# First mixer of a two-block transformer kernel: step size at unit xbc 6, SiLU calls in a row, attention weightings and decay sums further on

## The chip, the cores and the metric

The kernel runs on one core of a Trainium2 chip. The metric is the device time in microseconds; the median of three runs of the kernel before is 944.78 us. A core has TensorE for matmuls, which write to PSUM banks; VectorE, ScalarE and GpSimd for the rest; and queues of DMA transfers. Every engine works through its own instructions in the order in which the program issues them, and they meet only at semaphores. An engine that waits holds up all that is queued behind the waiting instruction.

## The reference

Two blocks, each a token mixer and a feed-forward part, on 256 tokens of width 1024, all in float32. The change lies in the mixer of the first block:

```python
proj = h @ w_in[l]
z, xbc, dt_raw, sb_qkv, nsa_q, nsa_kv, nsa_gate, merge_gate = jnp.split(proj, split_points(), axis=-1)
y_ssm = ssm_mixer(z, xbc, dt_raw, ...)           # state space
y_sb = stick_breaking_attention(sb_qkv)          # w = exp(ls + later), out = w @ v
y_nsa = nsa_attention(nsa_q, nsa_kv, nsa_gate, ...)
...
xbc = jax.nn.silu(causal_dwconv(xbc, conv_w, conv_b))     # in ssm_mixer
dt = jax.nn.softplus(dt_raw + dt_bias)                    # the step size
a = -jnp.exp(a_log)
...
decay = jnp.exp(jnp.where(tri, seg, -jnp.inf))            # per chunk of 128 tokens
w = cb[..., None] * decay * dt_c[:, None]                 # cb = C . B
y = y * silu(z); y = y * rsqrt(mean(y * y) + eps)         # per group of 256
```

The compression branch of `nsa_attention` makes one key and one value of 32 tokens each (`hid`, `kc` in the kernel), and a softmax over 15 of them (`cmp`).

## The kernel before, in words

The projection is cut into units of 256 columns of weights (1 MB each, streamed in through three slots). A float32 weight is split in two parts: ScalarE copies the rounded high part (`w_hi`, L1113), VectorE subtracts it to get the low part (`w_lo`, L1561), and TensorE makes three products for each pair of operands (L480 to L485), 48 matmuls a unit. `ahead(u)` on ScalarE and VectorE issues the splits up to two units on, so a split stands in each engine's queue at the place where the code calls `ahead`. A unit's result lies in one of three PSUM banks `pj`.

The order of units in the first mixer is sbq, sbk, sbv (attention), xbc 0 to 7, kk, kv, vv, nq 0 and 1, z 0 to 3, gm 0 to 11. It is the order of the weight stream and fixed. What stands between the units is written out by hand, once for each engine, and these four lists are what the change reorders. In them:

- `sb_scores`, `sb_later`, `sb_apply` (TensorE), `sb_logs`, `sb_exp`, `sb_hi` (ScalarE), `sb_keep`, `sb_sum`, `sb_mask`, `sb_lo` (VectorE) are the stick-breaking attention for head pair 0 or 1. `sb_apply` is the weighting of the values, L605 and L606; `sb_lo` reads its result last.
- `conv(i)` on VectorE takes unit xbc i from PSUM, issues a split (by `channel_major`, which calls `ahead`), and adds three taps for the even block (L1577); `conv_first(i)` on ScalarE issues a split and the first tap (L1198, L1204); `conv_odd(i)` on GpSimd adds three taps for the odd block (L384 to L390).
- the step size: `narrow_products` (24 matmuls into the bank `po`), `narrow_out`, `narrow_turn`, then `dtx`, `dt_e`, `dt_`, `dta` in tiny tiles.
- `silu(q)` activates four blocks of xbc; the transposes `xs` bring x to token order; `cb` are the products C . B; `seg(g)` are the decay sums (L713 to L716), `decay(g)` their exponential, `ssm_y(g)` the product with x.

Small results share three PSUM regions, S and T (two banks each of `pa`) and O (`po`). Lists of uses (`S_USE`, `T_USE`, `O_USE`) give each use its place, and `claim(pe, region, name)` makes TensorE wait until every use before it in the list has been read:

```python
k = USE[region].index(name)
if k:
    pe.wait_ge(S(f"{region}_read"), k)
```

Of the kernel before, what the change touches and what calls it, by code (L numbers as in the profile page):

```python
# [129 lines left out]
def program(nc, stream, params, consts, cmpw, gains, x_in, out):  # L130
    ctx = ExitStack()
    with ctx:
# [151 lines left out]
        O_USE = ["rbc0", "sb0", "sb1", "dt", "dt_tok", "y0", "y1", "y2", "y3", "t5", "hid", "kc"] \  # L284
# [181 lines left out]
        def _(pe):  # L466
# [224 lines left out]
            run_unit(("kk", 0))  # L691
            narrow_turn("dt_tok", 40)
# [53 lines left out]
            run_unit(("z", 1))  # L746
# [13 lines left out]
            run_unit(("z", 2))  # L760
# [5 lines left out]
            run_unit(("z", 3))  # L766
# [12 lines left out]
            run_unit(("gm", 0))  # L779
# [5 lines left out]
            run_unit(("gm", 1))  # L785
# [318 lines left out]
        def _(act):  # L1104
# [120 lines left out]

            act.wait_ge(S("prm_loaded"), 16)
            conv_first(0)
# [10 lines left out]
            sb_hi(1)  # L1238

            o = PCOLS["ws1"][0]  # L1240
            act.activation(ws_hi, prm[:, o:o + 320], ACT.Copy).then_inc(S("ws_hi"), 1)

            def silu(q):
                act.wait_ge(S("conv_even"), 2 * (q + 1))
                act.wait_ge(S("conv_odd"), 2 * (q + 1))
                act.activation(xbc[:, 4 * q:4 * q + 4, :], xbc[:, 4 * q:4 * q + 4, :], ACT.Silu)\
                   .then_inc(S("xbc_silu"), 1)

            silu(0)
            silu(1)  # L1250
            conv_first(6)
            conv_first(7)
            for q in range(4):
# [8 lines left out]
            ahead(("kk", 0))  # L1262
            silu(2)

            await_psum(act, "O", "dt_tok")
            read(act.activation(small40, po[:, 0:128].rearrange("p (b x) -> p b x", b=2)[:, :, 0:40], ACT.Copy), "O")
            act.activation(ea, prm_("a_log"), ACT.Exp).then_inc(S("ea_ready"), 1)
            act.wait_ge(S("dtx_ready"), 1)
            A.did(act.activation(dt_e, dtx, ACT.Abs))
            A.sync()  # L1270
            A.did(act.activation(dt_e, dt_e, ACT.Exp, scale=-1.0))
            A.sync()
            act.activation(dt_e, dt_e, ACT.Ln, bias=1.0).then_inc(S("dte_ready"), 1)
# [15 lines left out]

            decay(0)  # L1290
            token_major(("vv", 0), vv)
            decay(1)
            ahead(("nq", 0))
            decay(2)
            ahead(("nq", 1))
            decay(3)
            ahead(("z", 0))
            await_psum(act, "O", "t5")
            read(act.activation(t5_sb[0:4, :], po[0:4, 0:384], ACT.Copy), "O")
            token_major(("z", 0), z[:, :, 0:256])  # L1300
            token_major(("z", 1), z[:, :, 256:512])
# [3 lines left out]
            token_major(("z", 2), z[:, :, 512:768])  # L1305
# [5 lines left out]
            token_major(("z", 3), z[:, :, 768:1024])  # L1311
# [5 lines left out]
            ahead(("gm", 0))  # L1317
# [236 lines left out]
        def _(dve):  # L1554
# [124 lines left out]
            def conv(i):  # L1679
# [9 lines left out]
                for s_ in (1, 2, 3):  # L1689
# [603 lines left out]
```

## Time and profile before

| | us |
|---|---|
| median of three runs | 944.78 |
| profiled execution, own time | 944.75 |
| its span, first to last instruction | 943.0 |
| TensorE busy | 880.5 |
| VectorE busy | 598.0 |
| ScalarE busy | 480.5 |
| GpSimd busy | 136.1 |

In the rows below PE is TensorE, PEld its weight loads, DVE VectorE, ACT ScalarE, POOL GpSimd. A timeline row has the start in us from the span's begin, the duration, engine, line and operation, the output and inputs by tile and shape, how many instructions in a row are merged, and in brackets the idle time in front and what released it. Ends of matmuls are modelled: each reaches some 0.16 us over the next one's start, so that an idle time in brackets is that much shorter than the pause between starts. Most work tiles lie in one large tile called `area`.

### The profile page before, as it was taken

The page shows a single profiled execution, that of the slowest core. Times are in us where ns is not written, and L with a number is a line of the kernel's source. Part 1 is how long each engine was busy: PE and PEld are TensorE (multiplying, and loading weights), DVE is VectorE, ACT ScalarE, POOL GpSimd, SP SyncE. Part 2 cuts the span into 40 slices and gives each one's busy share as a digit, 9 for nine tenths or more (in the row PEclk, how much of TensorE's full clock was granted, in tenths as well). Part 3 has the DMA queues.
Part 4 walks back from the last instruction along what each step waited for, and adds up shares of the span by engine and source line. Part 5 has one row for each costly group of instructions (what it writes and reads, how often), then busy time and mean ns, then how long its engine had stood idle before and what let it go on. Part 6 is the DMA issues. An engine that isn't in the chain of part 4 may idle for free.

```text
span 943.0 us, 15727 instructions
## 1 busy us (share of the span) xinstructions
PE 880.5 (93%) x6246; PEld 813.5 (86%) x6246; DVE 598.0 (63%) x721; ACT 480.5 (51%) x692; POOL 136.1 (14%) x122
## 2 busy tenths in 40 slices
PE   3999888999999999898999999799998999999997
PEld 3999787999988998788899998688886799999995
DVE  4448756535777578666777777666545576655654
ACT  5356763236755534366666656464435344343332
POOL 0025661100000032023333233000000000000000
PEclk9999898999999999999999999799999999999999
DMA  8442333232432445544545465233321536555541
GB/s 328 158 179 91 134 134 134 88 122 105 146 138 108 157 149 191 196 170 145 185 174 187 178 221 181 90 134 134 135 90 68 178 113 223 179 178 183 193 157 45
DMA packets 21735, 143.82 MB, mean 153 GB/s; under 512 B 3008, under 2 KB 3012, under 8 KB 5168
## 3 DMA queue, kind: packets, MB, share of 16 engines
q1 hardware_dynamic: 19872, 138.30, 41.0%
q0 software_dynamic: 1808, 4.73, 1.4%
q8 instruction: 42, 0.69, 0.3%
q14 instruction: 13, 0.11, 0.0%
HBM read 141.96 MB, written 1.84 MB: 152 GB/s over the span
## 4 chain that ended last, share of the span: by engine, by line
PE 63%; DVE 14%; ACT 10%; issue 7%; POOL 4%; DMA 1%; ACTq 0%; SPq 0%; DVEq 0%; POOLq 0%
PE pj L480 12%; PE pj L483 9%; PE pj L482 9%; ACT w_hi L1113 4%; PE pa L875 4%; PE pa L876 4%; PE pa L877 4%; DVE w_lo L1561 4%; DVE area L1574 4%; POOL area L439 3%; DVE area L1577 3%; PE pj L484 2%; PE pj L485 2%; PE pa L519 2%; ACT area L1395 1%
## 5 line engine op out<-in xcount | busy, mean ns | idle before, releaser
L1561 DVE TENSOR_TENSOR w_lo<-w_raw,w_hi 128x2048 fp32r<-128x2048 f32 x128 | 303.4, 2373 | 92.1 <-ACT w_hi L1113 92.1
L480 PE MATMUL pj<-a_hi,w_hi 128*128 128x256 f32 x1184 | 341.4, 288 | 14.1 <-DVE w_lo L1561 10.0
L482 PE MATMUL pj<-a_lo,w_hi 128*128 128x256 f32 x1184 | 337.7, 285 | 0.0
L483 PE MATMUL pj<-a_hi,w_lo 128*128 128x256 f32 x1184 | 337.6, 285 | 0.0
L1113 ACT ACTIVATE w_hi<-w_raw 128x2048 fp32r<-128x2048 f32 x128 | 242.9, 1905 | 71.7 <-PE pa L877 38.6
L480 PEld LDWEIGHTS pj<-a_hi,w_hi 128*128 128x128 f32 x1184 | 230.2, 194 | 20.4 <-issue 17.8
L482 PEld LDWEIGHTS pj<-a_lo,w_hi 128*128 128x128 f32 x1184 | 230.1, 194 | 0.8
L483 PEld LDWEIGHTS pj<-a_hi,w_lo 128*128 128x128 f32 x1184 | 229.8, 194 | 0.0
L875 PE MATMUL pa<-w_hi,a_hi 128*128 128x512 f32 x280 | 110.1, 393 | 4.1 <-issue 2.5
L876 PE MATMUL pa<-w_lo,a_hi 128*128 128x512 f32 x280 | 109.9, 393 | 0.0
L877 PE MATMUL pa<-w_hi,a_lo 128*128 128x512 f32 x280 | 109.6, 391 | 0.0
L439 POOL TENSOR_TENSOR area<-area 128x255 f32<-128x255 f32 (+1 forms) x44 | 57.7, 1311 | 126.5 <-ACT area L1402 123.3
L1574 DVE TENSOR_TENSOR area<-pj,rbc 128x512 f32<-128x512 f32 x66 | 45.3, 686 | 45.0 <-PE pj L483 44.6
L875 PEld LDWEIGHTS pa<-w_hi,a_hi 128*128 128x128 f32 x280 | 53.1, 190 | 15.5 <-issue 5.1
L877 PEld LDWEIGHTS pa<-w_hi,a_lo 128*128 128x128 f32 x280 | 53.0, 189 | 11.2
L876 PEld LDWEIGHTS pa<-w_lo,a_hi 128*128 128x128 f32 x280 | 52.9, 189 | 10.2
L480 PE MATMUL pj<-w_hi,a_hi 128*128 128x256 f32 x176 | 51.8, 295 | 0.0
L484 PE MATMUL pj<-w_lo,a_hi 128*128 128x256 f32 x176 | 51.3, 291 | 0.0
L485 PE MATMUL pj<-w_hi,a_lo 128*128 128x256 f32 x176 | 51.1, 291 | 0.0
L1577 DVE SCALAR_TENSOR_TENSOR area<-area,prm 128x255 f32<-128x255 f32 (+2 forms) x68 | 46.4, 683 | 4.6 <-ACT area L1395 1.3
L1530 ACT ACTIVATE a_hi<-area 128x512 fp32r<-128x512 f32 x16 | 10.1, 632 | 73.7 <-DVE area L1577 73.7
L1352 ACT ACTIVATE area<-area,tiny 128x128 f32<-128x128 f32 (+1 forms) x64 | 28.4, 444 | 29.9 <-DVE tiny L1885 29.9
(249 smaller groups left out, 1119.2 us busy)
## 6 DMA issues: line engine op xcount, KB each, us to landing
w_raw<-stream SPq DMA_DIRECT2D x128, 1024.0 KB, 4.8
area<-gains POOLq DMA_DIRECT2D x4, 512.0 KB, 4.1
cst<-consts SPq DMA_DIRECT2D x1, 1093.0 KB, 13.4
x_tok<-x_in SPq DMA_DIRECT2D x2, 512.0 KB, 4.4
area<-cmpw POOLq DMA_DIRECT2D x1, 1024.0 KB, 5.4
out<-x_tok SPq DMA_DIRECT2D x4, 256.0 KB, 2.0
t_wide<-t_rows POOLq DMA_DIRECT2D x1, 768.0 KB, 13.1
prm<-params SPq DMA_DIRECT2D x1, 562.5 KB, 10.0
```

Source lines behind the costliest of these rows:

```text
L439: gp.tensor_tensor(facc[:, 1, s_:T], facc[:, 1, s_:T], tap[:, s_ - 1, 0:T - s_], ALU.add)\
L480: pe.matmul(out_, a[0], a[1], start=first, stop=False)
L482: pe.matmul(out_, wh, al, start=False, stop=False)
L483: return pe.matmul(out_, wl, ah, start=False, stop=last)
L484: pe.matmul(out_, ah, wl, start=False, stop=False)
L875: pe.matmul(o_, a_hi[:, chunk + kc, rows], w_hi[:, slot, c:c + 512], start=first, stop=False)
L876: pe.matmul(o_, a_hi[:, chunk + kc, rows], w_lo[:, slot, c:c + 512], start=False, stop=False)
L877: return pe.matmul(o_, a_lo[:, chunk + kc, rows], w_hi[:, slot, c:c + 512], start=False, stop=last)
L1113: act.activation(w_hi[:, slot, :], w_raw[:, slot, :], ACT.Copy).then_inc(S("w_hi_done"), 1)
L1561: dve.tensor_tensor(w_lo[:, slot, :], w_raw[:, slot, :], w_hi[:, slot, :].bitcast(F32), ALU.subtract)\
L1574: return dve.tensor_tensor(o_, a, b, op)
L1577: return dve.scalar_tensor_tensor(out=o_, in0=a, scalar=s_, in1=b, op0=op0, op1=op1)
```

## The change

It changes the four hand-written lists and one mask.

- TensorE: the first weighting stands behind unit xbc 4 (was 3), the second behind xbc 7 (was 5); the step-size products come right behind the first weighting (were behind xbc 6), their turn behind xbc 6 (was behind kk); the second `sb_later` comes behind these products; kk stands ahead of the transposes of x, vv ahead of the first decay sums. From there to gm 2 every small piece stands one unit later against the unit stream. `O_USE` gets the new order.
- ScalarE: the step-size activations come ahead of SiLU 0, and the four SiLU calls stand with fewer table changes between them; the copies of x follow SiLU 3; the high half of the small weights comes first.
- VectorE: `conv` is cut in `conv_out` and `conv_taps`; `sb_sum(0)`, `sb_keep(1)`, `sb_lo(0)`, `narrow_out`, `sb_lo(1)`, the step size, kk and kv move; the low half of the small weights comes first.
- The attention mask is applied to the two diagonal blocks of three; the third has ones in the mask.

```diff
-        O_USE = ["rbc0", "sb0", "sb1", "dt", "dt_tok", "y0", ...
+        O_USE = ["rbc0", "sb0", "dt", "dt_tok", "sb1", "y0", ...
@@ TensorE
             run_unit(("xbc", 3))
+            run_unit(("xbc", 4))
             await_value(pe, ("sbv", 0))
             await_value(pe, ("sbv", 1))
             sb_apply(0)
-            run_unit(("xbc", 4))
-            sb_later(1)
-            run_unit(("xbc", 5))
-            sb_apply(1)
-            run_unit(("xbc", 6))
             claim(pe, "O", "dt")
             pe.wait_ge(S("ws_ready"), 1)
             narrow_products(40)
+            sb_later(1)
+            run_unit(("xbc", 5))
+            run_unit(("xbc", 6))
+            narrow_turn("dt_tok", 40)
             run_unit(("xbc", 7))
+            sb_apply(1)
+            run_unit(("kk", 0))
...
+            run_unit(("vv", 0))
             seg(0)
-            for g, n in enumerate((("vv", 0), ("nq", 0), ("nq", 1), ("z", 0))):
+            for g, n in enumerate((("nq", 0), ("nq", 1), ("z", 0), ("z", 1))):
...
-            run_unit(("z", 3))
+            run_unit(("gm", 0))
             claim(pe, "S", "cmp")
...
-            run_unit(("gm", 0))
+            run_unit(("gm", 1))
             claim(pe, "T", "cmp")
@@ ScalarE
             conv_first(3)
+            conv_first(4)
             sb_hi(0)
-            conv_first(4)
             sb_exp(1)
+            act.activation(ea, prm_("a_log"), ACT.Exp).then_inc(S("ea_ready"), 1)
             conv_first(5)
+            conv_first(6)
...
+            act.activation(dt_e, dt_e, ACT.Ln, bias=1.0).then_inc(S("dte_ready"), 1)
             silu(0)
             silu(1)
-            conv_first(6)
             conv_first(7)
+            sb_hi(1)
+            silu(2)
+            ahead(("kk", 0))
+            silu(3)
@@ VectorE
+            tt(ws_lo, prm[:, o:o + 320], ws_hi.bitcast(F32), ALU.subtract).then_inc(S("ws_ready"), 1)
             conv(0)
             dve.wait_ge(S("cst_loaded"), 16)
             sb_keep(0)
             conv(1)
-            conv(2)
+            conv_out(2)
             sb_sum(0)
+            conv_taps(2)
             sb_mask(0)
+            conv(3)
             sb_keep(1)
-            conv(3)
+            conv(4)
             sb_lo(0)
-            conv(4)
+            narrow_out("dt", 40)
             sb_sum(1)
             sb_mask(1)
             conv(5)
-            sb_lo(1)
             conv(6)
...
+            conv_out(7)
             dve.wait_ge(S("dte_ready"), 1)
...
+            conv_taps(7)
+            sb_lo(1)
+            dve.wait_ge(S("conv_odd"), 7)
+            channel_major(("kk", 0), kk)
@@ masks (also in sb_mask)
-                tt(sb_lk[p], sb_lk[p], cst_("sbmask").unsqueeze(1).to_broadcast([P, 2, 384]), ALU.mult)\
+                tt(outer_blocks(sb_lk[p]), outer_blocks(sb_lk[p]), sb_diag, ALU.mult).then_inc(S("sb_lk_ready"), 1)
```

TensorE around the first weighting (L605, L606), before; L480 with `pj1` is the first matmul of unit xbc 4, L636 the first of the second `sb_later`, L480 with `pj2` the first of xbc 5:

```order
L605 MATMUL po<-area 128x256 [waits O_read,sb_w_ready,pj_read2,pj_read1]
L606 MATMUL po<-area 128x128
L605 MATMUL po<-area 128x256
L606 MATMUL po<-area 128x128
L480 MATMUL pj1<-a_hi,w_hi 128x256 [waits pj_read1,w_lo_done,w_hi_done]
...
L636 MATMUL pa<-area,cst 128x256 [waits sb_lk_ready,T_read]
...
L480 MATMUL pj2<-a_hi,w_hi 128x256 [waits pj_read2,w_lo_done,w_hi_done]
```

The same place now; L480 with `po` is the first of the 24 step-size products:

```order
L480 MATMUL pj1<-a_hi,w_hi 128x256 [waits pj_read1,w_lo_done,w_hi_done]
...
L605 MATMUL po<-area 128x256 [waits O_read,sb_w_ready,pj_read2,pj_read1]
L606 MATMUL po<-area 128x128
L605 MATMUL po<-area 128x256
L606 MATMUL po<-area 128x128
L480 MATMUL po<-a_hi 40x256 [waits ws_ready,O_read]
...
L636 MATMUL pa<-area,cst 128x256 [waits sb_lk_ready,T_read]
...
L480 MATMUL pj2<-a_hi,w_hi 128x256 [waits pj_read2,w_lo_done,w_hi_done]
```

The step-size products, with their wait for `O_read`, now stand between the weighting and the units from xbc 5 on; unit xbc 4 stands ahead of both.

VectorE up to `sb_lo(0)` (the row that writes `a_lo<-po`), before, from the mask of head pair 0 on:

```order
L1574 TENSOR_TENSOR area<-area,cst 128x768 [waits sb_exp_ready]
L1577 SCALAR_TENSOR_TENSOR area<-pa,area 128x768 [waits sb_log_ready]
L1574 TENSOR_TENSOR area<-area,pa 128x768 [waits dve_order]
L1574 TENSOR_TENSOR area<-area,cst 128x768 [waits S_read]
L1574 TENSOR_TENSOR area<-pj0,rbc 128x512 [waits unit_done,conv_odd,conv_tap3]
L1561 TENSOR_TENSOR w_lo<-w_raw,w_hi 128x2048 [waits w_hi_done]
L1577 SCALAR_TENSOR_TENSOR area<-area,prm 128x255 [waits conv_tap3,pj_read0]
...
L1574 TENSOR_TENSOR a_lo<-po,a_hi 128x512 [waits y_hi]
```

And now:

```order
L1571 TENSOR_TENSOR area<-area,cst 128x2x2x128 [waits sb_exp_ready]
L1571 TENSOR_TENSOR area<-pj0,rbc 128x512 [waits unit_done,conv_odd,conv_tap3]
L1558 TENSOR_TENSOR w_lo<-w_raw,w_hi 128x2048 [waits w_hi_done]
L1574 SCALAR_TENSOR_TENSOR area<-area,prm 128x255 [waits conv_tap3,pj_read0]
...
L1574 SCALAR_TENSOR_TENSOR area<-pa,area 128x768 [waits sb_log_ready]
...
L1571 TENSOR_TENSOR area<-pj1,rbc 128x512 [waits unit_done,conv_odd,conv_tap3]
L1558 TENSOR_TENSOR w_lo<-w_raw,w_hi 128x2048 [waits w_hi_done]
L1574 SCALAR_TENSOR_TENSOR area<-area,prm 128x255 [waits conv_tap3,pj_read1]
...
L1571 TENSOR_TENSOR a_lo<-po,a_hi 128x512 [waits y_hi]
```

conv(3) now stands ahead of `sb_keep(1)`, and conv(4) with its split and taps has come ahead of `sb_lo(0)`.

## Rows read from the trace of the kernel before

**Rows 1.** Page: busy us (share of the span) xinstructions by engine

```profile
PE 880.5 (93%) x6246; PEld 813.5 (86%) x6246; DVE 598.0 (63%) x721; ACT 480.5 (51%) x692; POOL 136.1 (14%) x122
```

**Rows 2.** Timeline of PE, first mixer: pieces and stalls up to seg(0)

```profile
77.38 0.36 PE L480 MATMUL pj<-a_hi,w_hi 128*128 128x256 f32 x1
...
84.76 0.67 PE L605 MATMUL po<-area 128*128 128x256 f32 x2 [1.39 <-DVE area L1574]
...
86.06 0.36 PE L480 MATMUL pj<-a_hi,w_hi 128*128 128x256 f32 x1
...
104.05 1.19 PE L605 MATMUL po<-area 128*128 128x256 f32 x2 [4.49 <-DVE area L1574]
...
113.66 0.28 PE L480 MATMUL po<-a_hi 128*40 128x256 f32 x1
...
116.47 0.28 PE L480 MATMUL pj<-a_hi,w_hi 128*128 128x256 f32 x1
...
145.91 0.80 PE L713 MATMUL pa<-cst,area 128*128 128x256 f32 x1 [6.70 <-DVE area L1574]
```

**Rows 3.** Windows: stretch, length, busy of PE, PEld, DVE, ACT, POOL, clock, DMA

```profile
102.59:109.41 6.82, 5.36 (x21) 5.03 (x22) 6.75 (x8) 5.61 (x9) 5.17 (x5) 0.50 0.29 86
143.55:150.37 6.82, 4.46 (x15) 3.92 (x16) 5.10 (x5) 3.66 (x6) 0.00 (x0) 0.50 0.53 172
...
245.95:249.36 3.41, 3.41 (x16) 3.41 (x17) 3.24 (x4) 3.41 (x3) 0.00 (x0) 0.50 0.48 197
```

**Rows 4.** Timeline of ACT: last tap of conv_first(2), sb_exp(0), split of xbc 5

```profile
80.96 0.51 ACT L1204 ACTIVATE area<-area,prm 128x256 f32<-128x256 f32 x1 [2.37 <-POOL area L384]
...
82.78 0.84 ACT L1218 ACTIVATE area<-area 128x768 f32<-128x768 f32 x1
...
87.26 1.90 ACT L1113 ACTIVATE w_hi<-w_raw 128x2048 fp32r<-128x2048 f32 x1
```

**Rows 5.** Timeline of DVE: sb_keep(1), split, taps, sb_lo(0)

```profile
87.39 0.96 DVE L1577 SCALAR_TENSOR_TENSOR area<-pa,area 128x768 f32<-128x768 f32 x1 [2.78 <-ACT area L1214]
...
90.85 2.28 DVE L1561 TENSOR_TENSOR w_lo<-w_raw,w_hi 128x2048 fp32r<-128x2048 f32 x1
93.05 2.10 DVE L1577 SCALAR_TENSOR_TENSOR area<-area,prm 128x255 f32<-128x255 f32 x3
95.07 0.68 DVE L1574 TENSOR_TENSOR a_lo<-po,a_hi 128x512 fp32r<-128x512 f32 x1
```

**Rows 6.** Timeline of POOL: adds of conv_odd(0) and (1); product of x and D

```profile
67.56 0.63 POOL L390 TENSOR_TENSOR area<-area 128x254 f32<-128x254 f32 x1
...
77.74 2.42 POOL L390 TENSOR_TENSOR area<-area 128x254 f32<-128x254 f32 x1
...
138.36 3.62 POOL L411 TENSOR_TENSOR area<-area,prm 128x2048 f32<-128x2048 f32 x1 [1.16 <-DVE area L1574]
```

**Rows 7.** Timeline of DVE: x by step size, a split, masks of C . B

```profile
134.21 4.07 DVE L1574 TENSOR_TENSOR area<-area,tiny 128x1024 f32<-128x1024 f32 x2
...
138.90 5.22 DVE L1561 TENSOR_TENSOR w_lo<-w_raw,w_hi 128x2048 fp32r<-128x2048 f32 x1
144.05 1.81 DVE L1574 TENSOR_TENSOR area<-pa,cst 128x1024 f32<-128x1024 f32 x2
```

**Rows 8.** Timeline of DVE: compression scores, product with z, norm of y

```profile
223.86 0.49 DVE L1574 TENSOR_TENSOR area<-pa,cst 128x128 f32<-128x128 f32 x2 [3.49 <-PE pa L775]
...
228.83 2.29 DVE L1574 TENSOR_TENSOR area<-area 128x2048 f32<-128x2048 f32 x1
...
237.33 2.29 DVE L1574 TENSOR_TENSOR area<-area,tiny 128x2048 f32<-128x2048 f32 x1
```

**Rows 9.** Timeline of PE: compression scores, transposes of y, next scores

```profile
221.34 2.48 PE L775 MATMUL pa<-tiny,area 64*128 64x16 f32 x32
...
241.35 1.91 PE L519 MATMUL pa<-cst,area 128*128 128x128 f32 x16
...
245.01 0.50 PE L594 MATMUL pa<-area 64*128 64x128 f32 x4 [1.75 <-DVE a_lo L1577]
```

More of the change, by code:

```diff
@@ L1224, in sb_hi, with silu @@
                        .then_inc(S("y_hi"), 1)
+            def silu(q):
+                act.wait_ge(S("conv_even"), 2 * (q + 1))
+                act.wait_ge(S("conv_odd"), 2 * (q + 1))
+                act.activation(xbc[:, 4 * q:4 * q + 4, :], xbc[:, 4 * q:4 * q + 4, :], ACT.Silu)\
+                   .then_inc(S("xbc_silu"), 1)
             act.wait_ge(S("prm_loaded"), 16)
+            o = PCOLS["ws1"][0]
+            act.activation(ws_hi, prm[:, o:o + 320], ACT.Copy).then_inc(S("ws_hi"), 1)
             conv_first(0)
@@ L1233, in _ @@
             conv_first(3)
+            conv_first(4)
             sb_hi(0)
-            conv_first(4)
             sb_exp(1)
+            act.activation(ea, prm_("a_log"), ACT.Exp).then_inc(S("ea_ready"), 1)
             conv_first(5)
[L1238 to L1247, printed above, removed]
+            conv_first(6)
+            await_psum(act, "O", "dt_tok")
+            read(act.activation(small40, po[:, 0:128].rearrange("p (b x) -> p b x", b=2)[:, :, 0:40], ACT.Copy), "O")
+            act.wait_ge(S("dtx_ready"), 1)
+            A.did(act.activation(dt_e, dtx, ACT.Abs))
+            A.sync()
+            A.did(act.activation(dt_e, dt_e, ACT.Exp, scale=-1.0))
+            A.sync()
+            act.activation(dt_e, dt_e, ACT.Ln, bias=1.0).then_inc(S("dte_ready"), 1)
             silu(0)
             silu(1)
-            conv_first(6)
             conv_first(7)
+            sb_hi(1)
+            silu(2)
+            ahead(("kk", 0))
+            silu(3)
+            act.activation(gate, small40[:, :, 16:40], ACT.Tanh, scale=0.5).then_inc(S("gate_tanh"), 1)
             for q in range(4):
@@ L1310, in _ @@
             read(act.activation(vrep, po[:, 64:128], ACT.Copy, scale=0.5), "O")
-            token_major(("z", 3), z[:, :, 768:1024])
+            ahead(("gm", 0))
             for b in set(BANK[("z", i)][0] for i in range(4)):
@@ L1316, in _ @@
             act.activation(cmp_e, cmp_e, ACT.Exp).then_inc(S("cmp_exp"), 1)
-            ahead(("gm", 0))
+            ahead(("gm", 1))
             await_psum(act, "T", "cmp")
@@ L1677, in narrow_out, with conv_out @@
                 read(tt(narrow[0:n, :], po[0:n, 0:T], rbc[0:n, :], ALU.mult), "O")
-            def conv(i):
+            def conv_out(i):
                 if i >= 2:
@@ L1698, in conv, with outer_blocks @@
                         V_.sync()
+            def conv(i):
+                conv_out(i)
+                conv_taps(i)
+            sb_diag = cst_("sbmask")[:, 0:P].unsqueeze(1).unsqueeze(1).to_broadcast([P, 2, 2, P])
+            def outer_blocks(t_):
+                return t_.rearrange("p a (b c) -> p a b c", c=P)[:, :, 0:3:2, :]
             def sb_keep(p):
@@ L1802, in _ @@
             ahead(("vv", 0))
+            ssm_w(0)
+            channel_major(("nq", 0), nq[:, 0:2, :], 64.0 ** -0.5)
             ssm_out(0)
             ssm_w(1)
-            channel_major(("nq", 0), nq[:, 0:2, :], 64.0 ** -0.5)
+            channel_major(("nq", 1), nq[:, 2:4, :], 64.0 ** -0.5)
             ssm_out(1)
             ssm_w(2)
-            channel_major(("nq", 1), nq[:, 2:4, :], 64.0 ** -0.5)
+            ahead(("z", 0))
             ssm_out(2)
             ssm_w(3)
-            ahead(("z", 0))
+            ahead(("z", 1))
             ssm_out(3)
-            ahead(("z", 1))
+            ahead(("z", 2))
             dve.wait_ge(S("hid_tanh"), 1)
@@ L1824, in _ @@
                .then_inc(S("hid_ready"), 1)
-            ahead(("z", 2))
+            ahead(("z", 3))
             await_read(dve, "O", "kc")
@@ L1828, in _ @@
                cst_("cmpmask").unsqueeze(2).to_broadcast([P, 8, 64]), ALU.mult).then_inc(S("cmp_v_ready"), 1)
-            ahead(("z", 3))
+            ahead(("gm", 0))
             await_psum(dve, "S", "cmp")
@@ L1861, in gm_copy @@
                               .rearrange("p (a t) -> p a t", a=2))
-            ahead(("gm", 0))
+            ahead(("gm", 1))
             await_read(dve, "O", "kc")
```

56 lines of the change are left out of this document (17 added, 39 removed).

## The prediction

> **What bounds the kernel now.** I read the page's busy line first: TensorE works 880.5 of 943.0 us, VectorE 598.0, ScalarE 480.5 [rows 1]. So the time is TensorE's work, which the change does not touch (the same matmuls in another order), plus the places where it stands idle or runs at the half clock. Then I listed TensorE's timeline for the first mixer and looked only for idle in front of a row. The reader is to see three stalls: 1.39 us before the first attention weighting (L605 at 84.76), 4.49 before the second (104.05), 6.70 before the first decay sums (L713 at 145.91), all released by VectorE, 12.6 us together [rows 2]. The third view is a table of windows: after the two long stalls the granted clock is 0.50 (1.2 GHz instead of 2.4), with 5.36 and 4.46 us of matmul work inside [rows 3]. In the window from 245.95 sixteen matmuls take 3.41 us, 0.213 each; at full clock 24 take 116.47 - 113.66 = 2.81, 0.117 each [rows 2, 3]. Work at the half clock loses about 0.45 of its time: 2.4, 2.0 and 1.5 us in the three windows. Last I read ScalarE's, VectorE's and GpSimd's timelines between these stalls, since they say what TensorE will wait for once its order is another.
>
> **The change part by part.** Durations are those of the profiled execution (span 943.0, own time 944.75; the three timed runs have their median at 944.78, so the sum stands for both).
>
> *Split of the small weights moved to the front.* One ScalarE copy and one VectorE subtraction of 320 elements (the nearest row is 0.51 for 256 [rows 4]), while both stand in front of the first xbc unit waiting for TensorE; cost 0. *Masks on two blocks of three:* 512 elements instead of 768, about 0.3 of 0.96 us each, four times; the two in front of the stalls count, and I carry them in the chains. *Two table loads fewer on ScalarE* and the freed VectorE slots: no place where either ends last, except in the chains below.
>
> *Weighting 0 behind unit xbc 4.* Unit xbc 3 starts at 77.38 and a unit lasts 5.8, so xbc 4 runs from 83.2 to 89.0. The weights are ready near 84 (the exponential at 82.78 takes 0.84, then the mask), so the 1.39 goes. The weighting lasts 86.06 - 84.76 = 1.30 [rows 2]: TensorE is at 90.3.
>
> *Step-size products next: the new wait.* They write the bank `po`, whose last reader is the low half of weighting 0 (`sb_lo(0)`). In VectorE's new queue that stands behind conv(3), sb_keep(1) and conv(4). conv(3) contains the weight split of unit xbc 5, which needs ScalarE's high half, and ScalarE's order there is unchanged: it comes free for the exponential at 82.8 after GpSimd's late tap (row at 80.96), and starts that split at 87.26, done 89.1 [rows 4]. All this comes 0.25 earlier by the shorter mask, so 88.9. From there VectorE works without a gap. From [rows 5]: split 2.2, three taps 2.0, sb_keep 2.65 (87.39 to 90.25 less the mask's 0.2), conv output 0.6, split 2.2, taps 2.0, `sb_lo` 0.65 = 12.3, that is 101.2; before, it ended at 95.75. TensorE idles 10.9, by the profile's way of counting 10.8. No earlier stall of this size is in the trace; from below it is 9.0 (GpSimd's add takes 2.42 us at 77.74 and 0.63 at 67.56 [rows 6]; undisturbed, it starts everything 1.8 earlier), from above 12.
>
> *Weighting 1 behind xbc 7.* Its 4.49 goes: the mask is ready near 110.6, the matmul arrives at 125.6. Chain of TensorE from 101.2: products 2.8, 5.0 at the half clock; later sums 1.7; xbc 5 from 108, xbc 6, turn of the step size, xbc 7 to 125.6; weighting to 126.9; kk to 132.7; the 16 transposes to 134.3. The VectorE and ScalarE splits for them are in time: the tightest is kv's. The step-size chain starts on VectorE only behind conv(6) (124.6), ScalarE runs exponential, logarithm, two SiLUs and then this split (to 132.1), VectorE to 134.3: cost 0 to 0.5, I take 0. TensorE is at 140.2.
>
> *The C·B products.* They claim both banks, so they wait for the four copies of x, now behind SiLU 3, which waits for GpSimd's last tap (about 138.6: five steps of mostly 0.6 to 1, behind ScalarE's at 133.1): copies to 141.8, idle 1.5. A wait of 0.3 stood here before, so 1.2 more. If GpSimd's last add meets VectorE's split, as at 77.74, it is 2 more.
>
> *First decay sums.* cb and unit vv bring TensorE to 150.35. VectorE: products of x and step 2.4 (two of 1024 at the rate of 0.96 for 768; the row shows 4.07, where GpSimd worked beside it), behind GpSimd's late decay product (142.7) = 145.1; kv's output; then its split, which sits behind GpSimd's 3.62 us product as in the row of 5.22 us, to 151.0; masks 1.7: 152.8 [rows 6, 7]. Idle 2.5, counted 2.3, in place of 6.70. Range 1 to 5.
>
> The Trainium skill, *SBUF — State Buffer*, section "Who interferes with whom", says that a VectorE instruction with both inputs in SBUF and a GpSimd one that reads SBUF block each other for the whole instruction, whoever starts first. By that rule the 5.22 is 3.1 of waiting and 2.1 of work, the trace agrees, and the 4.07 would be 2.4 plus waiting. Without the rule I would leave 4.07 and add 1.6 us here.
>
> Idle up to here: 10.8 + 1.2 + 2.3 = 14.3 against 12.6, **+1.7**. Clock: before 2.4 + 2.0 = 4.4; after 2.2 (4.8 us at half) + 1.5 = 3.7, **-0.7**.
>
> *z and gm units one place later.* Relative to z 3's end the compression scores now stand behind gm 0. Before, the scores started at 221.34, VectorE took them at 223.86, and its product with z (`y_gated`) followed them in its queue at 228.83; the normed y was done at 239.6, and TensorE came for it at 241.35, 1.7 later [rows 8, 9]. Now the scores start 6.4 later (0.6 for `kc`, 5.8 for gm 0); the exponential no longer queues behind z's SiLU, an estimated 1.55 back (0 to 1.6); and ScalarE's squares stand behind the copy of the turned scores, which waits for gm 1, 0.9 more. Sum 5.75: normed y 24.0 after z 3's end, while TensorE is there after 6.4 + 2.4 + 5.8 + 0.1 + 5.8 = 20.6. Idle 3.3, counted **+3.1**. The 1.75 behind it (245.01) stays. The half-clock window there grows, by 0 to 1.5: **+0.7**. Below, the cover of 1.7 and a quicker ScalarE could leave 1.5 of the 3.1; above, 4.5.
>
> Sum 1.7 - 0.7 + 3.1 + 0.7 = +4.8: 944.75 + 4.8 = **949.5**.
>
> **Rivals.**
> *Faster, VectorE reaches `sb_lo(0)` in time.* If it got there before TensorE (by 90.3), 10.9 go: 938.6. At the old end of 95.75, 5.45 go: 944.1, no change. The sum is 0 at 96.4, and under the measurable from 94.5 on. For it: the stalls of 4.49 and 6.70 do go. Against: nine instructions stand in order ahead, each with a row, and the first waits for ScalarE at a point that the change does not move.
> *Same: y is not late.* If the normed y came in time, 3.1 and 0.7 go: 945.7 (0.1% over). For it 1.7 of cover; against: the shift is 5.75.
> *Slower still.* GpSimd and VectorE meet at the last tap (+2) and at the decay product (+1.6), and the half clock lasts 3.4 us longer (+1.5): 954.6 with all, 952 with one.
> *The change does nothing where the stalls are:* excluded, the orders differ on every engine.
>
> **How the numbers follow.** Forecast 0.57 (947 to 952); slower still 0.14; y in time 0.12; `sb_lo(0)` at about its old end 0.05; earlier than that, so faster, 0.12. A measurement of this kernel tells about 0.2% (1.9 us) from no change. That gives faster 0.12, same 0.17 (y in time and the old end), slower 0.71. Range 943.5 to 953.5: it takes in the rival with the old end of `sb_lo(0)` and leaves out the best case and the sum of all collisions. The forecast's own range is 947 to 952.
>
> **What the new profile would show.** The first product of the step size (L480, `po<-a_hi`) with some 10 us of idle, released by VectorE, and a granted clock of 0.50 around it; no idle before either weighting; the C·B products with about 1.5, the decay sums with 1 to 5; the 16 transposes of y (L519) with about 3. It is wrong if the first stall is under 6 us, or y's transposes do not wait. A total under 943 would mean the first.

## The result, and the profile after

The changed kernel takes 951.63 us (median of 10 runs, 946.06 to 952.11), the kernel before 943.43 on the same chip (10 runs, 939.15 to 945.13). The ratio is 1.0081, with a 95% interval of 1.0058 to 1.0105: slower, by 0.8%. The difference of the medians is 8.2 us. The profiled execution of the changed kernel (its longest of the ten) has a span of 950.3 us and an own time of 952.11; before it was 943.0 and 944.75, so the two profiles to be compared are 7.36 us apart.

The busy line of the page, against [rows 1]:

```profile
span 950.3 us, 15727 instructions
PE 882.8 (93%) x6246; PEld 814.5 (86%) x6246; DVE 595.7 (63%) x721; ACT 477.6 (50%) x690; POOL 135.4 (14%) x122
```

TensorE has the same 6246 matmuls and is busy 2.3 us longer; the rest of the span's 7.3 is idle time. Windows over the first mixer and over what follows it say where (columns as in [rows 3]; the first two rows are of the kernel before, the last two of the changed one):

```profile
50.00:262.00 212.00, 196.59 (x1565) 190.91 (x1565) 128.64 (x137) 117.52 (x161) 56.19 (x48) 0.95 0.36 127
262.00:943.00 681.00, 648.16 (x4427) 587.66 (x4425) 446.83 (x560) 342.94 (x509) 79.72 (x70) 0.98 0.44 154
```

```profile
50.00:262.00 212.00, 192.11 (x1508) 185.74 (x1507) 120.33 (x128) 109.52 (x148) 57.44 (x48) 0.93 0.34 123
262.00:950.30 688.30, 655.48 (x4489) 594.42 (x4487) 452.87 (x568) 348.03 (x521) 77.77 (x70) 0.98 0.44 154
```

Window less busy TensorE is its idle time: 15.4 us in the first mixer before, 19.9 after, and 32.8 behind it in both. The whole span has 5.0 us of new idle time (67.5 against 62.5); 4.5 of it lie in the first mixer, and the granted clock there fell from 0.95 to 0.93. TensorE's timeline after has the stalls that answer to [rows 2] and [rows 9]:

```profile
89.36 0.59 PE L605 MATMUL po<-area 128*128 128x256 f32 x2
101.76 0.44 PE L480 MATMUL po<-a_hi 128*40 128x256 f32 x1 [10.93 <-DVE a_lo L1571]
...
106.58 0.59 PE L636 MATMUL pa<-area,cst 128*128 128x256 f32 x2
...
126.03 0.60 PE L605 MATMUL po<-area 128*128 128x256 f32 x2
...
144.77 3.78 PE L698 MATMUL pa<-area 128*128 128x256 f32 x8 [3.54 <-ACT area L1268]
...
156.04 0.38 PE L713 MATMUL pa<-cst,area 128*128 128x256 f32 x1
...
248.28 2.46 PE L519 MATMUL pa<-cst,area 128*128 128x128 f32 x16 [3.18 <-DVE area L1571]
...
251.97 0.81 PE L594 MATMUL pa<-area 64*128 64x128 f32 x4 [1.23 <-DVE a_lo L1574]
```

Neither weighting waits, nor do the decay sums. In their place stand the step-size products (10.9), the C . B products (3.5) and y's transposes (3.2). What the decay sums need from VectorE, the masks of C . B, is ready at 154.8, 1.3 us before TensorE comes:

```profile
152.98 1.80 DVE L1571 TENSOR_TENSOR area<-pa,cst 128x1024 f32<-128x1024 f32 x2
```

VectorE's queue is what the first of them waits for; the rows answer to [rows 5]:

```profile
89.26 2.29 DVE L1558 TENSOR_TENSOR w_lo<-w_raw,w_hi 128x2048 fp32r<-128x2048 f32 x1 [4.25 <-ACT w_hi L1113]
91.47 2.08 DVE L1574 SCALAR_TENSOR_TENSOR area<-area,prm 128x255 f32<-128x255 f32 x3
93.47 0.94 DVE L1574 SCALAR_TENSOR_TENSOR area<-pa,area 128x768 f32<-128x768 f32 x1
...
96.84 2.27 DVE L1558 TENSOR_TENSOR w_lo<-w_raw,w_hi 128x2048 fp32r<-128x2048 f32 x1
99.04 2.07 DVE L1574 SCALAR_TENSOR_TENSOR area<-area,prm 128x255 f32<-128x255 f32 x3
101.03 0.68 DVE L1571 TENSOR_TENSOR a_lo<-po,a_hi 128x512 fp32r<-128x512 f32 x1
```

The low half of weighting 0 (`a_lo<-po`) is the last reader of the bank that TensorE wants; it ends at 101.71. VectorE works all the time from 89.26; it is not slow, the short row simply stands last. The windows in which the clock was 0.50 in the first mixer, after:

```profile
95.95:106.19 10.24, 4.43 (x21) 3.83 (x22) 5.68 (x7) 3.31 (x6) 4.78 (x5) 0.50 0.29 104
143.73:150.56 6.83, 5.79 (x19) 5.07 (x20) 5.71 (x5) 2.99 (x5) 3.85 (x2) 0.50 0.61 252
205.17:208.58 3.41, 3.41 (x15) 2.91 (x14) 0.48 (x1) 2.28 (x2) 0.61 (x1) 0.50 0.03 7
232.48:235.89 3.41, 3.41 (x19) 3.41 (x18) 2.76 (x8) 2.21 (x2) 0.00 (x0) 0.50 0.04 10
249.55:256.37 6.82, 5.59 (x28) 4.54 (x26) 5.95 (x10) 6.82 (x11) 0.00 (x0) 0.50 0.01 4
```

Busy TensorE in them is 4.43 + 5.79 + 3.41 + 3.41 + 5.59 = 22.6 us. Before it was 5.36 + 4.46 + 3.41 [rows 3] and one more of 3.41, which the rows ahead of the prediction do not show:

```profile
198.16:201.57 3.41, 3.41 (x18) 3.41 (x17) 0.85 (x1) 2.53 (x4) 1.67 (x2) 0.50 0.01 2
```

That is 16.6. At the 0.45 of the prediction the 6.0 more of half-clock work cost 2.7 us, and 4.5 + 2.7 = 7.2 of the 7.36. This is a sum for the two profiled executions; how far half-clock time differs between executions of one kernel is taken up behind the experiments.

### The profile page after: what moved, and what is told of

It is laid out like the page before. It is cut to its first block, busy times and chain, and to the rows that moved or that the text cites. A ratio compares the mean times of both kernels' runs of the same rounds, so it can differ in the third digit from the quotient of the medians.

```text
span 950.3 us, 15727 instructions
## 1 busy us (share of the span) xinstructions
PE 882.8 (93%) x6246; PEld 814.5 (86%) x6246; DVE 595.7 (63%) x721; ACT 477.6 (50%) x690; POOL 135.4 (14%) x122
## 4 chain that ended last, share of the span: by engine, by line
PE 63%; DVE 12%; ACT 11%; issue 8%; POOL 4%; DMA 1%; ACTq 0%; DVEq 0%; SPq 0%; POOLq 0%
PE pj L480 12%; PE pj L483 9%; PE pj L482 9%; ACT w_hi L1113 5%; PE pa L875 4%; PE pa L876 4%; PE pa L877 4%; DVE area L1574 3%; DVE w_lo L1558 3%; DVE area L1571 3%; POOL area L439 3%; PE pj L484 2%; PE pj L485 2%; PE pa L519 2%; PE pj L575 1%
## 5 line engine op out<-in xcount | busy, mean ns | idle before, releaser
L1558 DVE TENSOR_TENSOR w_lo<-w_raw,w_hi 128x2048 fp32r<-128x2048 f32 x128 | 303.4, 2373 | 101.2 <-ACT w_hi L1113 101.2
L480 PE MATMUL pj<-a_hi,w_hi 128*128 128x256 f32 x1184 | 341.3, 288 | 14.2 <-DVE w_lo L1558 9.8
L480 PEld LDWEIGHTS pj<-a_hi,w_hi 128*128 128x128 f32 x1184 | 229.8, 194 | 21.1 <-issue 18.4
L439 POOL TENSOR_TENSOR area<-area 128x255 f32<-128x255 f32 (+1 forms) x44 | 55.7, 1267 | 128.5 <-ACT area L1399 125.3
L877 PEld LDWEIGHTS pa<-w_hi,a_lo 128*128 128x128 f32 x280 | 53.0, 189 | 11.3
L876 PEld LDWEIGHTS pa<-w_lo,a_hi 128*128 128x128 f32 x280 | 53.1, 190 | 10.1
L480 PE MATMUL pj<-w_hi,a_hi 128*128 128x256 f32 x176 | 52.1, 296 | 0.0
L1527 ACT ACTIVATE a_hi<-area 128x512 fp32r<-128x512 f32 x16 | 10.1, 632 | 73.7 <-DVE area L1574 73.7
```

What stands on the lines that cost most here:

```text
L439: gp.tensor_tensor(facc[:, 1, s_:T], facc[:, 1, s_:T], tap[:, s_ - 1, 0:T - s_], ALU.add)\
L480: pe.matmul(out_, a[0], a[1], start=first, stop=False)
L876: pe.matmul(o_, a_hi[:, chunk + kc, rows], w_lo[:, slot, c:c + 512], start=False, stop=False)
L877: return pe.matmul(o_, a_lo[:, chunk + kc, rows], w_hi[:, slot, c:c + 512], start=False, stop=last)
L1558: dve.tensor_tensor(w_lo[:, slot, :], w_raw[:, slot, :], w_hi[:, slot, :].bitcast(F32), ALU.subtract)\
```

## The experiments

The table has all ten; times are in us. "Idle" and "clock" are of the one profiled execution of each kernel. "Idle" is TensorE's idle time in the first mixer (window 50 to 262; where a kernel is early, a wait of 0.94 us that stands behind 262 in the others is taken off), "clock" the granted clock of that window. Kernels of different groups ran on different chips, so the ratio to the kernel before on the same chip is the one to compare.

| kernel | median (runs) | ratio and interval | own time, profiled | idle | clock |
|---|---|---|---|---|---|
| before | 943.43 (10) | 1 | 944.75 | 15.4 | 0.95 |
| after | 951.63 (10) | 1.0081 (1.0058 to 1.0105) | 952.11 | 19.9 | 0.93 |
| e1: `sb_lo(0)` early | 937.88 (12) | 0.9966 (0.9945 to 0.9987) | 941.06 | 14.3 | 0.98 |
| e2: y early | 946.05 (8) | 1.0057 (1.0035 to 1.0080) | 943.55 | 17.3 | 0.94 |
| e3: kk's output after the add | 946.32 (11) | 1.0072 (1.0049 to 1.0095) | 947.02 | 20.8 | 0.94 |
| e4: e1 and e2 | 937.70 (12) | 0.9960 (0.9942 to 0.9978) | 939.54 | 9.7 | 0.95 |
| e5: e4, products behind xbc 5 | 934.12 (6) | 0.9921 (0.9901 to 0.9942) | 935.67 | 8.7 | 0.97 |
| e6: e4, copies ahead of SiLU 3 | 934.36 (6) | 0.9932 (0.9909 to 0.9955) | 934.00 | 9.5 | 0.98 |
| e7: e4, e5, e6 | 929.35 (4) | 0.9872 (0.9846 to 0.9898) | 930.41 | 8.4 | 1.00 |
| e8: before, mask alone | 940.38 (1) | one run | 940.38 | 14.6 | 0.96 |
| e9: after, 85 matmuls in the wait | 970.06 (6) | 1.0297 (1.0269 to 1.0325) | 970.59 | 4.6 | 0.97 |
| e10: after, 24 matmuls in the wait | 946.14 (12) | 1.0042 (1.0023 to 1.0061) | 946.58 | 10.1 | 0.98 |

**e1, the low half of weighting 0 ahead of conv(4).** The large stall by itself.

```diff
@@ ScalarE
-            conv_first(4)
             sb_hi(0)
+            conv_first(4)
@@ VectorE
             conv(3)
+            sb_lo(0)
             sb_keep(1)
             conv(4)
-            sb_lo(0)
```

> The changed kernel with one thing moved: the copy of the first weighting to its high part stands ahead of the first taps of xbc 4 on ScalarE, and its low half ahead of sb_keep(1) and conv(4) on VectorE. Theory (the 10.9 us stall at the step-size products is the wait for the reader of their bank, which stood behind two blocks of work): the low half ends at 94.1 instead of 101.7, the idle time falls from 10.9 to 3.5, and the stalls behind do not grow, since their chains start from the products: 7 us and one stretch of half clock less, 944 to 945 where the changed kernel has 952. Rival (VectorE is the bound of this whole stretch, and whoever is served first only moves the wait): sb_keep(1) and the split of xbc 6 come 0.7 later, the second later sums or unit xbc 6 wait instead, total idle time in front of xbc 7 stays over 9 us, 951 to 952.

Measured: 0.9966, faster than the kernel before. First PE's row, then VectorE's:

```profile
93.79 0.31 PE L480 MATMUL po<-a_hi 128*40 128x256 f32 x1 [3.37 <-DVE a_lo L1571]
```

```profile
88.84 2.29 DVE L1558 TENSOR_TENSOR w_lo<-w_raw,w_hi 128x2048 fp32r<-128x2048 f32 x1 [4.25 <-ACT w_hi L1113]
91.05 2.08 DVE L1574 SCALAR_TENSOR_TENSOR area<-area,prm 128x255 f32<-128x255 f32 x3
93.06 0.68 DVE L1571 TENSOR_TENSOR a_lo<-po,a_hi 128x512 fp32r<-128x512 f32 x1
```

The wait is 3.4 us instead of 10.9. Of that 7.5, 1.4 come back at the decay sums and 0.5 at the scores behind y, so idle falls by 5.6. The profile is 11.05 us shorter, more than expected: work at the half clock is 10.2 us instead of 22.6, another 12.4 x 0.45 = 5.6. By the ratios the move is worth 1.2%, 10.8 us, so the whole loss of the change goes with most of this one stall; in the profiled executions half of that is clock.

**e2, y's product with z ahead of the compression scores.** The second predicted term by itself.

```diff
@@ ScalarE, ahead of the squares and the root of y
-            ahead(("gm", 1))
-            await_psum(act, "T", "cmp")
-            read(act.activation(pct, pt[:, 0, 0:T], ACT.Copy), "T")
@@ VectorE, ahead of the scores of cmp (was behind them)
+            dve.wait_ge(S("z_silu"), 1)
+            await_read(dve, "O", "y3")
+            tt(y_tok, y_tok, z, ALU.mult).then_inc(S("y_gated"), 1)
```

(The three lines of ScalarE now stand behind the root, and VectorE's own `ahead(("gm", 1))` goes, since `gm_copy` issues that split.)

> The changed kernel with y's product with z ahead of the compression scores on VectorE, and y's squares and root ahead of the copy of the turned scores and of one weight split on ScalarE; all other work the same. Theory (the 3.2 us stall at the transposes of y comes from the scores, one unit later, standing ahead of y in both queues): y is normed at 19 to 20 us after z 3's end instead of 24, TensorE comes at 20.6, the idle time of 3.2 goes to 0 to 0.3 and its half clock with it: 3 to 5 us less, 947 to 949. Rival (y waits for its own chain, SiLU of z, squares, root): the transposes still wait 2 us or more, 950.5 to 952.

Measured: 1.0057. y's transposes do not wait any more (3.18 to 0), the next scores wait 1.75 instead of 1.23, as they did before the change [rows 9]; idle falls by 2.6. In idle time the term is as predicted. The intervals of e2 and of the changed kernel overlap, so the total alone does not show it. Nor does the length of the profile, 8.6 us shorter: 2.6 of that are idle time, 3.1 are what less half-clock work in the first mixer saves (15.7 us instead of 22.6), and 2.5 what less of it behind 262 us saves (13.1 instead of 18.6), where the edit changes nothing.

**e3, kk's output waits for GpSimd's last add.** For the collision at the last tap: in the changed kernel the add meets VectorE's split.

```diff
             sb_lo(1)
-            dve.wait_ge(S("conv_odd"), 7)
+            dve.wait_ge(S("conv_odd"), 8)
             channel_major(("kk", 0), kk)
```

> The changed kernel with one constant: VectorE waits for GpSimd's last tap of xbc 7 before it takes kk and splits vv's weights (it waited for the one of xbc 6). Theory (that add took 2.56 us because the split was on its way): the add takes 0.63, SiLU 3 starts 1.9 earlier, the idle time before the C.B products falls from 3.5 to 1.5. VectorE's masks come no earlier, since GpSimd's product and the split of nq 0 still meet, so 1 to 3 us of idle time appear before the decay sums: together 0.5 to 1.5 less, 950.5 to 951.5. Rival (the add is slow for another reason): it stays near 2.5 and the total does not move, or rises by the wait of 1.

The changed kernel's last add, then e3's:

```profile
138.93 2.56 POOL L384 TENSOR_TENSOR area<-area 128x253 f32<-128x253 f32 x1
```

```profile
138.40 0.63 POOL L384 TENSOR_TENSOR area<-area 128x253 f32<-128x253 f32 x1
```

The add takes 0.63 and the C . B products wait 1.6 instead of 3.5: the collision was worth the 1.9 that the rival put at 2. But the split now starts behind the add and meets GpSimd's next step, the decay product:

```profile
139.68 4.33 DVE L1558 TENSOR_TENSOR w_lo<-w_raw,w_hi 128x2048 fp32r<-128x2048 f32 x1
```

```profile
139.93 1.92 POOL L405 TENSOR_TENSOR area<-cst,tiny 128x1024 f32<-128x1024 f32 x1
```

The split takes 4.33 instead of 2.54, and the decay sums, which had not waited, wait 3.0. The idle time is 0.9 more than in the changed kernel. The totals overlap and do not tell the two apart. e3's profile is 5.1 us shorter than the changed kernel's in spite of its idle time, and 4.7 of that come from behind 262 us, out of the edit's reach: 8.2 us of half-clock work there instead of 18.6 (the stretch at 0.50 that lasts 10.24 us from 604.53 in the changed kernel lasts 6.83 from 603.80 in e3, and those at 700.10 and 734.24 have no counterpart). Between two single executions a difference of this size need not come from the edit. A collision that is only put off is found again one step on.

**e4, e1 and e2 together.** Do the two terms add?

> Both reorderings together: the low half of the first weighting early, and y ahead of the compression scores. Theory: the two savings add, 7 and 3 to 5 us: 939 to 942, faster than the kernel before. Rival for each part as for the single runs; if VectorE bounds the first stretch, 947 to 949.

In idle time they do: 19.9 - 5.6 - 2.6 = 11.7 was due, 9.7 is left (2.0 less: the decay sums' 1.4 is not there, and the 0.5 at the scores stood in both). Where the 1.4 went is in these rows, e1's first. The masks end 10.0 us after the first C . B product in both; in e4 the clock behind the C . B wait is 0.50, and TensorE comes 11.4 us after that product instead of waiting:

```profile
134.86 0.70 PE L698 MATMUL pa<-area 128*128 128x256 f32 x2 [3.56 <-ACT area L1268]
144.94 0.48 PE L713 MATMUL pa<-cst,area 128*128 128x256 f32 x1 [1.44 <-DVE area L1571]
```

```profile
134.81:141.64 6.83, 6.06 (x20) 5.34 (x21) 5.98 (x5) 2.96 (x5) 3.85 (x2) 0.50 0.57 236
146.97 0.38 PE L713 MATMUL pa<-cst,area 128*128 128x256 f32 x1
```

So the half clock took the place of the wait: 2.7 us longer work for 1.4 us of idle time.

In the total the two terms do not add: 0.9960 is e1's ratio within either interval. In the profiled executions the granted clock says why: e4 has five stretches at 0.50 with 19.6 us of work, e1 three with 10.2. But that is one execution of each. e4's twelve lie in two groups of six, 933.46 to 935.87 us with a mean granted clock of 0.981 to 0.987, and 939.54 to 939.90 with 0.970 to 0.978; the profiled one is of the second (939.54, 0.970). The 19.6 us belong to that execution, and it is not shown that the order brings them.

**e5, unit xbc 5 ahead of the step-size products.** e4's remaining 3.4 in front of them should be covered by a unit.

```diff
+            run_unit(("xbc", 5))
             claim(pe, "O", "dt")
             pe.wait_ge(S("ws_ready"), 1)
             narrow_products(40)
             sb_later(1)
-            run_unit(("xbc", 5))
             run_unit(("xbc", 6))
```

> The kernel with both reorderings, and in TensorE's list unit xbc 5 ahead of the step-size products (they stand right behind it now, ahead of the second later sums). Theory (each piece waits only for its own inputs: xbc 5 for its low half at 91.5, the products for the low half of the first weighting at 94.1): 0.6 to 1.0 us of idle before xbc 5 and none before the products, in place of 3.4; the later sums start 6 us later and unit xbc 7 waits 0 to 0.5 for its split: idle time 7 to 7.5 us in the first mixer where the kernel with both reorderings has 9.7, total 2 us less, 935 to 937. Rival (the step size has to be early, that is what the change is for): the turn, SiLU 0 and 1 and kv's split come 3 us or more later against TensorE, and kv, the C.B products or the decay sums wait that much more: total the same or 1 to 2 us more.

Measured: 934.12 against the expected 935 to 937. The 3.4 is gone, but xbc 5 itself waits 0.82 for its split (row below), two other units wait 1.1 together and a weighting 0.7, so that idle is 8.7 and not 7 to 7.5. The profile is 3.9 us shorter than e4's with 1.0 less idle time; the rest is clock, with the same caution as for e4. The intervals of the ratios of e4 and e5 just touch.

```profile
90.11 0.35 PE L480 MATMUL pj<-a_hi,w_hi 128*128 128x256 f32 x1 [0.82 <-issue]
```

**e6, the four copies of x ahead of SiLU 3.** For the C . B products, which wait for these copies.

```diff
             ahead(("kk", 0))
-            silu(3)
-            act.activation(gate, small40[:, :, 16:40], ACT.Tanh, scale=0.5)...
             for q in range(4):
                 ...                          # the copies of x
+            silu(3)
+            act.activation(gate, small40[:, :, 16:40], ACT.Tanh, scale=0.5)...
```

> The kernel with both reorderings, and on ScalarE the four copies of x ahead of SiLU 3 (and of the tanh of the gate) instead of behind. Theory (the 3.55 us before the C.B products are GpSimd's last tap, SiLU 3 and then 2.0 us of copies, in a row): the copies fill the wait for the tap, idle time before C.B falls by 1.9 to 2.0, and the decay sums do not wait, or less than 1: idle 7.7 to 8.7 in the first mixer instead of 9.7. Rival (GpSimd's products and VectorE's splits lock each other later on and the decay sums wait in its place): idle stays 9 to 10.

The wait is 1.6 instead of 3.5, and as the rival said most of it comes back: the decay sums wait 1.67, behind a VectorE product that now meets GpSimd's:

```profile
128.35 2.54 DVE L1558 TENSOR_TENSOR w_lo<-w_raw,w_hi 128x2048 fp32r<-128x2048 f32 x1
130.81 4.49 DVE L1571 TENSOR_TENSOR area<-area,tiny 128x1024 f32<-128x1024 f32 x2
```

In the changed kernel the same two products took 2.36 (at 144.85, with GpSimd idle). Idle fell by 0.2 only. Yet the profile is 5.5 us shorter than e4's: 6.8 us of work at the half clock instead of 19.6, 12.8 x 0.45 = 5.8. Between these two executions nothing was won but the clock. That the move won it is not shown: e6's six executions (933.0 to 937.2) lie where e4's shorter six do, and the intervals of the two ratios overlap.

**e7, all four moves.**

> All of it: both reorderings, xbc 5 ahead of the step-size products, copies of x ahead of SiLU 3. Theory: the savings add, idle 5 to 6 us in the first mixer (15.4 in the kernel before, 19.9 in the changed one), 933 to 936. Rival: the two later moves compete for the same chain, idle 7 or more, no better than one of them.

Its waits in the first mixer (releaser; us in total, times, longest), and its window:

```profile
PE pj L480 <- issue: 1.9, 3, 0.9
PE pa L594 <- DVE a_lo L1574: 1.7, 1, 1.7
PE pa L713 <- DVE area L1571: 1.7, 1, 1.7
PE pa L698 <- ACT area L1229: 1.6, 1, 1.6
PE pa L519 <- DVE area L1906: 0.9, 1, 0.9
PE po L746 <- DVE area L1571: 0.8, 1, 0.8
PE po L605 <- ACT tiny L1250: 0.7, 1, 0.7
```

```profile
50.00:262.00 212.00, 202.69 (x1674) 196.06 (x1673) 137.07 (x158) 123.06 (x179) 57.48 (x48) 1.00 0.39 136
```

It is 1.3% faster than the kernel before, and the best of all: its interval lies below every other one. The idle time is 8.4, not the expected 5 to 6, and the total is nevertheless lower than expected: no stretch at 0.50 is left in the first mixer. The two parts account for its whole distance to the changed kernel: idle 19.9 - 8.4 = 11.5, clock 22.6 x 0.45 = 10.2, together 21.7, and 952.11 - 930.41 = 21.7. By the ratios, over all executions, the distance is 2.1%, 19.7 us.

**e8, the mask alone, on the kernel before.**

```diff
-                tt(sb_w[p], sb_w[p], cst_("sbmask")...to_broadcast([P, 2, 384]), ALU.mult)
+                tt(outer_blocks(sb_w[p]), outer_blocks(sb_w[p]), sb_diag, ALU.mult)
```

> The kernel before with the mask on two blocks of three and nothing else. Theory: each of the four masks takes 0.3 us less on VectorE (0.69 for 0.96), the chains in front of both weightings shorten by 0.3 to 0.6: idle time in front of them 1.39 and 4.49 falls to 0.8 to 1.1 and 3.9 to 4.3, total less by under 1.5, not to be told from noise in one run. Rival (the two-piece access runs at a lower rate): the masks take as long as before and nothing moves.

```profile
83.94 0.67 PE L605 MATMUL po<-area 128*128 128x256 f32 x2 [0.86 <-DVE area L1574]
...
102.97 1.19 PE L605 MATMUL po<-area 128*128 128x256 f32 x2 [4.24 <-DVE area L1574]
```

The mask takes 0.69 us instead of 0.96, the two weightings wait 0.86 and 4.24 instead of 1.39 and 4.49 [rows 2], the decay sums 6.7 as before. It is worth up to 0.8 us of idle, as expected.

**e9 and e10, matmuls in the long wait.** To price the half clock: TensorE works through the 10.9 us with products that nobody reads.

```diff
+            bank_free(*BANK[("xbc", 5)])
+            keep_warm(2, 24)                 # e9: 85
             claim(pe, "O", "dt")
```

> The changed kernel with 85 matmuls added whose result nobody reads (identity by 256 columns, into the bank of the coming unit xbc 5), between the first weighting and the step-size products: some 10 us of work in the 10.9 us of waiting. Theory (the wait costs its own length and a half clock behind it): the products start at the same moment, 101.8 or up to 0.3 later, the granted clock stays 1.00 around them (it was 0.50 from 95.9 to 106.2), they and the later sums take 2 us less; nothing else moves: total about 2 us less than the changed kernel, ratio to the kernel before 1.005 to 1.007 where the changed kernel had 1.008. Rival (the clock falls by its own schedule and not by what TensorE did): the clock is 0.50 there all the same and the total as before or up to 1 more.

> The changed kernel with 24 of the unread matmuls in the wait before the step-size products instead of 85: the run with 85 showed 0.43 us for each (two records of 0.215 at full clock), so 24 fill 10.3 of the 10.9 us. Theory (the wait costs its own length and the half clock behind it): the products start at 101.7 to 102, the granted clock is 1.00 around them, they and the later sums take about 2 us less than in the changed kernel, and the rest is as it was: ratio to the kernel before 1.005 to 1.007. Rival (the clock falls whatever TensorE does): 0.50 there as before, ratio 1.008 or more.

e9 (970.06, 3% over the kernel before) missed its question, since I had mis-sized the product: these plain float32 matmuls take 0.43 us each, in two records, and ran 25 us past the wait.

```profile
90.39 36.86 PE L531 MATMUL pj<-cst 128*128 128x256 f32 x170
```

e10 with 24 of them fits. TensorE is at the products at 100.80 and the clock there is full:

```profile
90.13 10.09 PE L531 MATMUL pj<-cst 128*128 128x256 f32 x46
100.80 0.31 PE L480 MATMUL po<-a_hi 128*40 128x256 f32 x1 [0.57 <-DVE a_lo L1573]
...
103.63 0.59 PE L636 MATMUL pa<-area,cst 128*128 128x256 f32 x2
```

```profile
101.50:106.20 4.70, 4.70 (x39) 4.55 (x38) 1.03 (x2) 0.00 (x0) 0.78 (x2) 1.00 0.20 82
```

From the first product to the later sums it is 2.83 us, in the changed kernel 106.58 - 101.76 = 4.82: the half clock behind the stall costs 2.0 us. The expected ratio was 1.005 to 1.007, the measured is 1.0042 (1.0023 to 1.0061), which barely meets the changed kernel's interval. In the three traces with this wait left empty (the changed kernel, e2, e3) the clock is 0.50 around the products, in the two with the wait filled (e9, e10) it is 1.00: the clock depends on what TensorE did in the wait, and not on the wait as such. The profile is 5.5 us shorter, more than the 2.0 at this place: the later stretches at 0.50 in the first mixer changed too, and all of them hold 10.2 us of work instead of 22.6. Whether the filled wait did that is not shown.

## Why the prediction was right, and which term was not

The forecast of 949.5 (slower) against 951.63, in the range. The direction and the largest stall came from the mechanism that was forecast. The total is 2.1 us off, the difference to the kernel before more: +8.2 by the medians where +4.8 was forecast. That the total is the closer one is luck, since the kernel before had a median 1.3 us under the time that the sum started from. Point by point:

- **Step-size products.** Predicted 10.8 of idle released by VectorE's `sb_lo(0)`, with products from 101.2: 10.92, from 101.76. The working was a sum of rows of before in a new order, and each row kept its length. Only the start was 0.4 late, 89.26 instead of 88.9: the shorter mask did not bring ScalarE's split forward (87.33, before 87.26). e1 takes most of the wait away by moving one short piece, and the loss with it: shown.
- **Weightings.** Predicted 0 each: 0 each. In front of kv, predicted 0: 0.24.
- **C . B products and decay sums.** Predicted 1.5 and 2.3, measured 3.54 and 0. The sum of the two was near (3.8 and 3.5), its parts were not. The rival's collision of GpSimd's last add took place, 2.56 us as in the row of 2.42 [rows 6]. TensorE came to the decay sums at 156.04 instead of 150.35: 0.9 by what had gathered before, 2.0 by the longer C . B wait, and 2.7 because C . B and unit vv took 11.3 us instead of 8.6, in good part at the half clock. The masks came at 154.8 instead of 152.8. With the 8.6 TensorE would have waited about 1.4, as it does in e1, where the C . B wait is the same and the clock behind it 1.00. The sum of the prediction took a stall of 2.3 and a half-clock term of 1.5 for the same place; there the one hides the other, and they do not add. e3 and e6 show the trade with the first wait: less in front of C . B, more in front of the decay sums.
- **The split behind GpSimd's product.** 5.23 us, in the row of 5.22 [rows 7]. The product of x and step size, which I put at 2.4 on the ground that GpSimd would be idle, took 2.36; in e6, beside GpSimd, 4.49. (At the rate named there, 0.96 for 768, two of 1024 come to 2.56 and not 2.4.) The Trainium skill, *SBUF — State Buffer*, section "Who interferes with whom", has this as an exclusive lock between a VectorE instruction with two inputs in SBUF and a GpSimd one that reads SBUF, and these rows agree. Which of the two starts first does not decide it in e3's rows as they stand: the split starts 0.25 us before the product and ends 2.2 us, its own length, behind the product's end.
- **y's transposes.** Predicted 3.1: 3.18. e2 takes it away by one move: shown. The scores behind them wait 1.23 instead of the 1.75 that I had left. The working has a slip here: TensorE's terms add up to 20.5 and not 20.6, so that the idle time would be 3.5 instead of 3.3.
- **The clock: the term that was mis-sized.** The sum had -0.7 for the two stalls and +0.7 at gm, together 0; measured it is +2.7. Piece by piece: behind the long stall 4.43 us of half-clock work (predicted 4.8; -0.4 us of time against before); behind C . B 5.79 instead of 4.46 (predicted less, +0.6); a new stretch at 232.48 behind the compression scores (not predicted, +1.5); at gm 5.59 instead of 3.41 (predicted +0.7, +1.0). I had put the clock down to the stalls, and also overlooked a fourth stretch of before at 198.16, which has a counterpart of the same size at 205.17. e10 shows that the first of these hangs on the stall; for the others no run shows a cause.

Idle was predicted at +4.8 and came out at +4.5; idle and clock together at +4.8 and +7.2. The rival "slower still" had the right kinds of surplus, a collision and a longer half clock, but what the two added in front of and behind C . B was in part taken back at the decay sums.

**What stays open.** Why a particular stretch at 0.50 falls where it does, and how much of it belongs to the order of the kernel. e4 has less idle time than e1 and more half-clock work, e6 the same idle time as e4 and a third of its half-clock work; e1 has no stretch at 0.50 behind its C . B wait of 3.6 us, e4 has one behind 3.5. Executions of one kernel spread by up to 10.8 us (e3; 6.0 in the changed kernel and in the one before). In e4 the longer ones have the lower mean granted clock. In the changed kernel the two shortest (946.06 and 946.20) have the lowest, 0.971, and its longest 0.973. The mean also counts stretches in which TensorE has little to do (e4's profile has 10.24 us at 0.50 from 11.93, with 4.0 us of matmuls), so it does not settle the matter, and only one execution of each kernel has a trace. That the clock makes the spread is therefore not shown. Nor is it shown which of e7's moves was the one that freed the clock.

## What to carry to other kernels

When pieces are moved past each other by hand, list for each claimed bank its last reader, and sum the rows that stand ahead of that reader in its own queue: here a row of 0.68 us behind 12 us of unrelated work cost 10.8 us by the ratios of the changed kernel and e1, where the rest of the change wins 3. Put the short last reader ahead of the long work. Then price TensorE's waits twice, once as idle time and once as half-clock work behind them: between the profiled executions of the changed kernel and of e7, idle made 11.5 us and the clock 10.2. Do not simply add the two: where TensorE waits for another engine's chain, half-clock work ahead of the wait fills it. And read half-clock time from several executions before an order is held responsible for it.

## What the runs showed of the hardware

- In the profiled execution of e7, whose single waits are 1.7 us at most and 8.4 together, the granted clock was 1.00 over the whole first mixer. Every other order had at least one wait of 3.4 us or more and stretches at 0.50, in e1 only from 194.5 and in e6 only from 218 us on, far behind their waits of 3.4 us at the step-size products. The runs do not tell the length of a wait from its place or from the sum of them.
- A plain float32 matmul of 256 columns took 36.86 / 85 = 0.43 us, in two records; the kernel's rounded products take 0.117 each [rows 2].
- The amount of half-clock work differed where the code was the same: behind 262 us it was 18.6 us in the changed kernel's profile, 13.1 in e2's and 8.2 in e3's.
- VectorE took 2.54, 4.33 and 5.23 us for splits of 2048 elements that alone take 2.28, by what GpSimd had under way. Both attempts to move one of the two (e3, e6) met the next instruction of the other.
